# A two-layer encoder with mixtures of experts: layer 1's experts with 64 rows and the high and low halves of x in one stationary operand

## The reference

```
def hier_moe(xn, w_group, b_group, w_expert, b_expert, w1, w3, w2):
    t = xn.reshape(-1, D_MODEL)                     # 384 x 1024
    ...                                             # top-1 of 4 groups, top-2 of its 4 experts
    gates = ...                                     # 384 x 16, two entries of a row are not zero
    y = jnp.zeros_like(t)
    for e in range(N_EXPERTS):                      # 16
        hdn = jax.nn.silu(t @ w1[e]) * (t @ w3[e])  # 512 wide
        y = y + gates[:, e:e + 1] * (hdn @ w2[e])
    return y.reshape(shp)
```

## Time and profile before

| | us |
|---|---|
| median of 3 runs | 1135.64 (1133.21 to 1136.66) |
| the profiled execution | 1134.98 |
| its span in the trace | 1133.3 |
| PE busy in the span | 1063.2 (94%) |
| DVE busy | 780.7 (69%) |
| ACT busy | 594.1 (52%) |
| POOL busy | 84.9 (7%) |
| mean granted clock of PE | 0.961 |

### The profile page before, as it was taken

The page is one execution under the profiler, slowest core; times in us unless marked ns, Lnnn a source line. Parts: engine busy times, 40 slices in busy tenths (PEclk is TensorE's granted clock), DMA queues, the critical chain, the costliest instruction groups (busy, mean ns, idle before and its releaser), DMA issues.

```text
span 1133.3 us, 13594 instructions
## 1 busy us (share of the span) xinstructions
PE 1063.2 (94%) x5197; PEld 770.8 (68%) x5197; DVE 780.7 (69%) x629; ACT 594.1 (52%) x462; POOL 84.9 (7%) x109
## 2 busy tenths in 40 slices
PE   5999999998999999999698977889999999999997
PEld 4889998786666666666486736776776666666664
DVE  4447564468689889898154455364778988888986
ACT  6236433253677777776232324134436777777770
POOL 5000000004000000000210200000030000000022
PEclk9999999998999999999799988698899999999999
DMA  9444442947899999994650103003578999999954
GB/s 352 141 150 149 141 149 75 374 164 281 327 373 400 388 386 402 389 399 184 224 188 1 39 1 149 1 0 153 219 270 327 374 387 383 396 398 389 404 192 164
DMA packets 44916, 279.88 MB, mean 247 GB/s; under 512 B 6392, under 2 KB 10904, under 8 KB 32184
## 3 DMA queue, kind: packets, MB, share of 16 engines
q1 hardware_dynamic: 33136, 240.21, 54.9%
q0 software_dynamic: 9216, 30.20, 7.8%
q10 hardware_dynamic: 2520, 8.85, 2.0%
HBM read 260.91 MB, written 18.50 MB: 247 GB/s over the span
## 4 chain that ended last, share of the span: by engine, by line
PE 84%; DVE 8%; ACT 4%; DMA 2%; issue 2%; ACTq 0%; SPq 0%; DVEq 0%
PE ps L188 30%; PE ps L194 15%; PE ps L526 4%; PE ps L580 4%; PE ps L623 3%; PE ps L1966 3%; PE ps L1940 3%; PE ps L586 2%; PE ps L534 2%; PE ps L630 1%; PE ps L1307 1%; PE ps L1923 1%; PE ps L1276 1%; DVE moe_wl L1084 1%; PE ps L1988 1%
## 5 line engine op out<-in xcount | busy, mean ns | idle before, releaser
L1084 DVE TENSOR_TENSOR raw_lo<-raw,moe_wh 128x4096 fp32r<-128x4096 f32 x48 | 212.4, 4425 | 44.0 <-ACT moe_wh L1079 43.9
L1084 DVE TENSOR_TENSOR moe_wl<-moe_raw,moe_wh 128x4096 fp32r<-128x4096 f32 x48 | 212.3, 4425 | 34.0 <-ACT moe_wh L1079 33.8
L188 PE MATMUL ps<-moe_wh,moe_xh 128*72 128x512 f32 x512 | 204.6, 400 | 5.1 <-DVE moe_xl L1179 4.8
L188 PE MATMUL ps<-moe_wh,moe_xl 128*72 128x512 f32 x512 | 202.6, 396 | 0.0
L1079 ACT ACTIVATE moe_wh<-raw 128x4096 fp32r<-128x4096 f32 x48 | 173.8, 3621 | 9.3 <-PE ps L2117 5.1
L1079 ACT ACTIVATE moe_wh<-moe_raw 128x4096 fp32r<-128x4096 f32 x48 | 173.7, 3620 | 3.8 <-DMA moe_raw<-in_moe_w_dram 3.8
L188 PEld LDWEIGHTS ps<-moe_wh,moe_xh 128*72 128x72 f32 x512 | 73.2, 143 | 49.5 <-DVE moe_xl L1179 5.8
L188 PEld LDWEIGHTS ps<-moe_wh,moe_xl 128*72 128x72 f32 x512 | 73.1, 143 | 43.2 <-issue 0.9
L328 DVE TENSOR_TENSOR raw_lo<-raw,gm_wh 128x4096 fp32r<-128x4096 f32 x12 | 53.1, 4426 | 70.2 <-ACT gm_wh L322 67.8
L188 PE MATMUL ps<-moe_wh,moe_hTh 128*72 128x512 f32 x256 | 81.9, 401 | 4.0 <-DVE moe_hTl L1184 3.3
L188 PE MATMUL ps<-moe_wh,moe_hTl 128*72 128x512 f32 x256 | 80.7, 397 | 0.0
(11 more groups left out here) (391 smaller groups left out, 1653.5 us busy)
## 6 DMA issues: line engine op xcount, KB each, us to landing
raw<-in_moe_w_dram SPq DMA_DIRECT2D x48, 2048.0 KB, 11.2
moe_raw<-in_moe_w_dram SPq DMA_DIRECT2D x48, 2048.0 KB, 11.3
raw<-in_gm_w_in_dram SPq DMA_DIRECT2D x7, 2048.0 KB, 8.1
moe_yrows<-moe_rows ACTq DMA_DIRECT2D x30, 288.0 KB
raw<-in_gm_w_out_dram SPq DMA_DIRECT2D x4, 2048.0 KB, 7.7
moe_rows<-moe_xrows POOLq DMA_DIRECT2D x28, 288.0 KB, 9.7
raw<-in_gm_w_in_dram SPq DMA_DIRECT2D x2, 1024.0 KB, 10.7
at_cache<-in_cache_ckv_dram SPq DMA_DIRECT2D x2, 1024.0 KB, 13.3
```

Source lines behind the costliest of these rows:

```text
L188: nc.tensor.matmul(out[c], x(t, k), wh[:, k, c * 512:c * 512 + 512], start=start and k == 0 and x is xh, stop=False)
L1084: nc.vector.tensor_tensor(w_lo[slot], w_raw[slot], w_hi[hi][:].bitcast(F32), ALU.subtract).then_inc(wl_ready, 1)
```

## The change

In layer 1 an expert has room for 64 rows (CAPS = (72, 64)). xh and xl of a slice lie side by side there, 64 + 64 columns, and form one stationary operand of 128 columns (`xwide`). Its product with wh puts the 64 rows of xh wh on partitions 0 to 63 of the bank and those of xl wh on 64 to 127; xh wl is added on partitions 0 to 63. A product of w1 or w3 in layer 1 so has 16 matmuls in place of 24. The two parts are then added outside PE: ACT copies partitions 64 to 127 to SBUF, DVE adds partitions 0 to 63; SiLU reads that sum and stands behind the sum of w3's copy in ACT's order. Two semaphores, `lower` and `summed`, tie these. w2 is as before, with 64 rows. The transfers of rows and results of layer 1 move 64 rows.

In both layers, `rows`, `hid` and the row table are kept in plain order: `weigh_rows` and the gate product read and write without a step, and PE reads with `by_slice` in the transposes of the router, of x and of `hid`, and in `gather_x`. EXTRA goes from 10 to 11, and one semaphore of the attention (`nw_ssq`) is merged with another (`nw_product`).

The core of the diff; most of the lines left out replace CAP by the layer's cap.

```diff
-CAP = 72
-EXTRA = SLOTS // (CAP + 1)
+CAPS = (72, 64)
+CAP = max(CAPS)
+EXTRA = SLOTS // (min(CAPS) + 1)
...
-        xsplit = [[sb(f"moe_x{p}{i}", [P, KD, CAP], F32R, moe) for p in "hl"] for i in range(2)]
+        xs = [sb(f"moe_x{i}", [P, 2 * KD * CAP], F32R, moe) for i in range(2)]
+        xsplit = [[[x[:, i * KD * CAP:(i + 1) * KD * CAP].rearrange("p (k t) -> p k t", k=KD) for i in range(2)] for x in xs],
+                  [[x[:, 0:KD * P].rearrange("p (k x t) -> p k x t", k=KD, x=2)[:, :, i] for i in range(2)] for x in xs]]
+        xwide = [x[:, 0:KD * P].rearrange("p (k t) -> p k t", k=KD) for x in xs]
...
-                g.dma_start(rows[0:CAP, par, :], xrows[bass.ds(row, CAP), :]).then_inc(x_loaded[par], 16)
+                g.dma_start(rows[0:cap, par, :], xrows[bass.ds(row, cap), :]).then_inc(x_loaded[par], 16)
...
-            nc.vector.tensor_tensor(rows[:, t].rearrange("q (k p) -> q k p", k=KD), by_slice(h[:, t], KD), by_slice(gain[:], KD),
-                                    ALU.mult).then_inc(rt_xn, 1)
+            nc.vector.tensor_tensor(rows[:, t], h[:, t], gain[:], ALU.mult).then_inc(rt_xn, 1)
...
                     last = nc.tensor.transpose(ps[:, ROW_BANK[l][t] + k // 4, (k % 4) * P:(k % 4 + 1) * P],
-                                               rows[:, t, k * P:(k + 1) * P], ident)
+                                               by_slice(rows[:, t], KD)[:, k], ident)
...
-                a.dma_start(yrows[bass.ds(row, CAP), :], rows[0:CAP, 2 + par, :]).then_inc(y_stored, 16)
+                a.dma_start(yrows[bass.ds(row, cap), :], rows[0:cap, 2 + par, :]).then_inc(y_stored, 16)
...
             def step(e, par, m):                       # ACT
                 a.wait_ge(w_used, M_MOE[l] + (1 if is_first(e) else 3 * e))
                 at_least(a, hid_done, E0 + e)
-                nc.scalar.activation(sil[:], ps[0:CAP, BA], ACT.Silu).then_inc(silu_done, 1)
-                if not is_first(e):
+                if l:
+                    nc.scalar.activation(sil[0:cap], ps[cap:P, BA], ACT.Copy).then_inc(lower, 1)
+                    if not is_first(e):
+                        hidden_high(e - 1)
+                    moe_split_h(a, l, *([3, 0, 3, 0] if is_first(e) else [3 * e + 2, 2, 5 if par else 2, m]))
+                    a.wait_ge(w_used, M_MOE[l] + (2 if is_first(e) else 3 * e + 1))
+                    nc.scalar.activation(hid[0:cap], ps[cap:P, BB], ACT.Copy).then_inc(lower, 1)
+                    a.wait_ge(summed, 2 * e + 1)
+                nc.scalar.activation(sil[0:cap], sil[0:cap] if l else ps[0:cap, BA], ACT.Silu).then_inc(silu_done, 1)
+                if not l and not is_first(e):
                     hidden_high(e - 1)
-                moe_split_h(a, l, *([3, 0, 3, 0] if is_first(e) else [3 * e + 2, 2, 5 if par else 2, m]))
+                if not l:
+                    moe_split_h(a, l, *([3, 0, 3, 0] if is_first(e) else [3 * e + 2, 2, 5 if par else 2, m]))
...
             def step(e, par, m):                       # DVE
+                if l:
+                    v.wait_ge(lower, 2 * e + 1)
+                    nc.vector.tensor_tensor(sil[0:cap], ps[0:cap, BA], sil[0:cap], ALU.add).then_inc(summed, 1)
                 if not is_first(e):
                     hidden_low(e - 1)
                 moe_split_l(v, l, *([3, 0, 3] if is_first(e) else [3 * e + 2, 2, 5 if par else 2]))
                 v.wait_ge(w_used, M_MOE[l] + (2 if is_first(e) else 3 * e + 1))
+                if l:
+                    v.wait_ge(lower, 2 * e + 2)
+                    nc.vector.tensor_tensor(hid[0:cap], ps[0:cap, BB], hid[0:cap], ALU.add).then_inc(summed, 1)
+                    v.wait_ge(summed, 2 * e + 2)
                 v.wait_ge(silu_done, E0 + e + 1)
-                nc.vector.tensor_tensor(hid[:].rearrange("q (k p) -> q k p", k=KE), by_slice(sil[:], KE), by_slice(ps[0:CAP, BB], KE),
-                                        ALU.mult).then_inc(hid_done, 1)
+                nc.vector.tensor_tensor(hid[0:cap], sil[0:cap], hid[0:cap] if l else ps[0:cap, BB], ALU.mult).then_inc(hid_done, 1)
...
-                                               rows[0:CAP, par, k * P:(k + 1) * P], ident[0:CAP, 0:CAP])
+                                               by_slice(rows[0:CAP, par], KD)[:, k], ident[0:CAP, 0:CAP])
                 last.then_inc(xT_done, 1)
+
+            def stacked_product(j, x, xh, wh, wl, bank):
+
+                pe.wait_ge(wh_ready, m0 + j + 2)
+                for k in range(KD - 1):
+                    nc.tensor.matmul(ps[:, bank], x[:, k], wh[:, k], start=k == 0, stop=False)
+                pe.wait_ge(wl_ready, m0 + j + 1)
+                for k in range(KD):
+                    nc.tensor.matmul(ps[0:cap, bank], xh[:, k], wl[:, k], start=False, stop=False)
+                return nc.tensor.matmul(ps[:, bank], x[:, KD - 1], wh[:, KD - 1], start=False, stop=True)
...
-                    last = nc.tensor.transpose(ps[:, BH, k * CAP:(k + 1) * CAP], hid[:, k * P:(k + 1) * P],
+                    last = nc.tensor.transpose(ps[:, BH, k * CAP:(k + 1) * CAP], by_slice(hid[:], KE)[:, k],
                                                ident[0:CAP, 0:CAP])
...
-                        last = nc.tensor.matmul(ps[:, BX + k // 4, (k % 4) * CAP:(k % 4 + 1) * CAP], rows[:, t, k * P:(k + 1) * P],
-                                                hot[:, e, t], start=t == 0, stop=t == TILES - 1)
+                        last = nc.tensor.matmul(ps[:, BX + k // 4, (k % 4) * CAP:(k % 4) * CAP + cap], by_slice(rows[:, t], KD)[:, k],
+                                                hot[:, e, t, 0:cap], start=t == 0, stop=t == TILES - 1)
```

More of the change, by code:

```diff
@@ L730, in build @@
         silu_done, hid_done = sem("silu_done"), sem("hid_done")
+        lower, summed = sem("moe_lower"), sem("moe_summed")
         hT_done, hh_ready, hl_ready = sem("hT_done"), sem("hh_ready"), sem("hl_ready")
@@ L802, in moe_sync @@
             load("moe_w2", NE - 1, 3 * NE - 1, S[5])
-            s = over[l]
+            s, cap = over[l], CAPS[l]
             sp.wait_ge(rt_table, l + 1)
@@ L815, in moe_sync @@
                     at_least(sp, s["st"], 16 * i + 16)
-                    sp.dma_start(rows[0:CAP, 0, :], xrows[bass.ds(row, CAP), :]).then_inc(s["x"], 16)
+                    sp.dma_start(rows[0:cap, 0, :], xrows[bass.ds(row, cap), :]).then_inc(s["x"], 16)
                     for slot, name in enumerate(("moe_w1", "moe_w3", "moe_w2")):
@@ L820, in moe_sync @@
                     at_least(sp, s["act"], 5 * i + 5)
-                    sp.dma_start(yrows[bass.ds(row, CAP), :], rows[0:CAP, 2, :]).then_inc(s["st"], 16)
+                    sp.dma_start(yrows[bass.ds(row, cap), :], rows[0:cap, 2, :]).then_inc(s["st"], 16)
             if l == 0:
@@ L847, in moe_pool @@
         def moe_pool(g, l):
+            cap = CAPS[l]
             if l == 0:
@@ L1335, in turn_kept @@
                 for t in range(TILES):
-                    nc.tensor.transpose(ps[0:CAP, BR, t * P:(t + 1) * P], hot[:, i, t], ident)
+                    nc.tensor.transpose(ps[0:cap, BR, t * P:(t + 1) * P], hot[:, i, t, 0:cap], ident)
                 for t in range(TILES):
-                    last = nc.tensor.matmul(ps[0:CAP, BR, TOK:TOK + 1], hot[:, i, t], kept_w[:, t, i:i + 1], start=t == 0,
+                    last = nc.tensor.matmul(ps[0:cap, BR, TOK:TOK + 1], hot[:, i, t, 0:cap], kept_w[:, t, i:i + 1], start=t == 0,
                                             stop=t == TILES - 1)
@@ L1344, in spread_y @@
                 for c in range(2):
-                    last = nc.tensor.matmul(ps[:, SPREAD[t][c]], kept_hot[:, i, t * P:(t + 1) * P],
+                    last = nc.tensor.matmul(ps[:, SPREAD[t][c]], kept_hot[0:cap, i, t * P:(t + 1) * P],
                                             kept_y[:, i, x, c * 512:c * 512 + 512], start=x == 0, stop=False)
@@ L1364, in moe_tensor @@
                     for c in range(2):
-                        last = nc.tensor.matmul(ps[:, SPREAD[t][c]], kept_hot[:, 1, t * P:(t + 1) * P].bitcast(F32),
-                                                rows[0:CAP, 3, c * 512:c * 512 + 512], start=False, stop=True)
+                        last = nc.tensor.matmul(ps[:, SPREAD[t][c]], kept_hot[0:cap, 1, t * P:(t + 1) * P].bitcast(F32),
+                                                rows[0:cap, 3, c * 512:c * 512 + 512], start=False, stop=True)
                     last.then_inc(spread, 1)
@@ L1382, in moe_tensor @@
                         for k in range(KD):
-                            last = nc.tensor.matmul(ps[0:CAP, bank], rows[:, 1, k * CAP:(k + 1) * CAP],
+                            last = nc.tensor.matmul(ps[0:cap, bank], rows[:, 1, k * cap:(k + 1) * cap],
                                                     moe_w_view(raw[:, slot], KD)[:, k], start=k == 0, stop=k == KD - 1)
@@ L1387, in moe_tensor @@
                     for k in range(KE):
```

(4 more changed lines are left out.)

114 lines of the change are left out of this document (59 added, 55 removed).

## The result

The changed kernel takes 1149.01 us (median of 4 runs, 1146.34 to 1152.75) against 1134.43 of the kernel before (4 runs): a ratio of 1.0133, 95% interval 1.0092 to 1.0174. The forecast was 1116. The time lies inside the stated range, which reaches up to 1156, but on the other side of the kernel before: the second rival, the dear stepped load, came true. The profiled execution took 1146.34 us, with a span of 1144.7 and a mean granted clock of 0.941.

What follows compares the result with a forecast made beforehand. PE and DMA were both taken as full at about 17.4 us an expert in layer 1. 1134.98 - 12.1 (loop) - 1.3 (start) - 2.5 (tail) - 2.2 - 0.8 (row weighting) = 1116 us; own range 1107 to 1128, stated range up to 1156.

Steps and rivals of the forecast that it cites:

- the second rival, the dear stepped load: PE's stepped loads on the path cost up to 47 us, giving 1163; chance 0.22 for dearer than break-even.
- the part on plain order: Row weighting gains 2.2 us in layer 1 and 0.8 in layer 0; PE's stepped loads taken as free.
- The upper bound, DVE's own ratio: PE's stepped loads at DVE's stepped pace: some 0.15 us more per transpose load, 0.12 per gather pass.
- the prediction's own counts: Stepped loads on the path: 12 x 15 transpose loads in layer 0, 2 x 84 gather passes, 348 together.
- row weighting: Weighting without a step on DVE: 0.8 us saved in layer 0, 2.2 in layer 1.
- break-even: From 54 ns more per stepped load the kernel is no longer faster; chance 0.06 for 40 to 64 ns.
- The rival of the clock: Layer 1's loop: PE idles before each w1 and the granted clock falls; 0.07 together with a stalled chain, 1128 and up.
- The stacked products: Layer 1: 16 fewer matmuls an expert save PE 3.7 us, from 17.42 to 13.7.
- the floor on DVE: Layer 1's loop: DVE's own work of 16.1 us an expert is the lower bound of the period.
- The mixture of that floor and of the DMA engines: Layer 1's period at 16.7 us, the middle of 16.1 and 17.27; 14 steps take 233.8 us, -12.1.
- The start of layer 1's experts: The second expert's w1 starts at 846.6 instead of 847.93, -1.3 us (0 to -1.3).
- The tail: End of layer 1: the last expert's shorter stacked products give -2.5 us (0 to -3.7).

Runs made afterwards that it cites:

- e4: The kernel before, plus blocks of PE work behind layer 0's first gather pricing loads at steps 1 to 8; 1262.97 us with the blocks.
- e7: e2 with row and result transfers of 16 rows, not 64, in layer 1 from the fifth expert on; 1122.73 us, ratio 0.9903.
- e2: The changed kernel with rows sorted by slice in both layers and `hid` sorted in layer 0 only; 1125.57 us, ratio 0.9919.
- e9: e2 with SP waiting for the end of the row scatter ahead of layer 1's eighth weight load; 1118.04 us, ratio 0.9866.

## Why the prediction was wrong

**The step that failed** is in the part on plain order: "I take nothing, since the nearest row is PE's own load". That row shows PE loading without a step, and so says nothing of a step; that PE's pace differs from DVE's was no ground for a price of zero. The upper bound, DVE's own ratio, gave 0.12 us for a gather pass, and 0.241 - 0.116 is 0.125. For a transpose it gave 0.15 where 0.043 was measured: the load of a transpose takes half of what that of a gather pass takes (116 against 242 ns at a step of 8 in e4). With the measured prices the prediction's own counts give 180 x 0.043 + 168 x 0.125 = 28.7 us, and 1116 + 28.7 = 1145, against 1146.3 in the profiled execution. That this is so close is in part luck, for the sum leaves out the clock and keeps 0.8 us of row weighting that never came. The mechanism was listed, and its place, its counts and its break-even were right; its price was taken at the lower of two ends, 0 and 47 us, and the measured one lies between them.

**What it left out** is the clock behind the gathers: the gathers were bounded by their passes alone, and the matmuls behind each were slower too (2.91 us for 1.67). The rival of the clock looked for a fall in front of each w1 in the loop; there the granted clock was 0.99 (881.5 to 1101).

**What was right.** The stacked products and the floor on DVE: 15.9 us an expert for 16.1, with DVE busy 99% of it. The mixture of that floor and of the DMA engines: 233.3 us for 14 steps where 233.8 were forecast; e7 shows both parts of it. That it came out so near is in part luck: the middle of two bounds was taken without a reason for the middle, and the same loop took 240.8 us in e2 and 231.5 in e9. The start of layer 1's experts without the stepped loads: -1.7 in e2 for -1.3. The tail: -3.8, and -2.3 in e2, for -2.5. Row weighting takes 1.23 us for 2.02 and gave 2.5 us in layer 1 for 2.2.

**What was off.** Row weighting gave nothing in layer 0 (forecast -0.8): the third tile's transposes start at 237.75 and 237.81 in the two kernels, behind PE's own work for the tiles ahead, though DVE was ready 0.9 earlier. And the forecast followed PE, DVE and the bytes of the weights, but not what an earlier release sets off: in e2 the weight loads collide with the scatter of rows, and the loop gives 5.0 where 12.1 were forecast. With the stepped loads gone and the collision out of PE's way, e9 stands at 1118; the forecast without row weighting's 3.0 was 1119.

## What to carry to other kernels

A permutation has to be paid on some engine at every read, so ask which engine is the bound in each stage that reads it: DVE's 0.8 us saved per tile cost PE 0.125 us in each of 192 gather passes. Where the trace has no row for the moved access, a row of the same engine without it is no lower price; the other engine's pace is the better guess (here right for a gather pass, 3.5 times too high for a transpose), and a few blocks like those of e4 price each kind of load. Expect the price in full where few moving columns follow a load. When a bound is removed, look for what its earlier end sets off: here weight loads that ran into a scatter whose rows were needed first, and one wait in the queue was worth 6 to 7 us.

## What the runs showed of the hardware

A stepped fp32 stationary load of 128 columns is hidden behind the 128 moving columns of a transpose (116 and 119 ns at steps of 1 and 8) and behind the 512 of a matmul pass (436 and 441), and not behind 72. A gather pass doubles from a step of 4 on (120 to 237 ns), a transpose of 72 rows pays at a step of 2 already (70 to 125 ns), and at a step of 8 half of what a pass takes (116 against 242 ns). The granted clock fell to 0.50 in stretches where PE was busy all the time, with passes held by such loads, and their pace stayed the same (a pass every 0.24 us). Two weight loads of 2 MB beside an indirect scatter delayed its end by some 12 us (from 3.5 to 15.2 behind the issue of its last piece), one by 7 (10.8).
